# RWKV-7 branch of a two-layer hybrid trunk: the masked key weights times the values, split by halves of the output tokens

## What is computed

```python
sa = jnp.einsum('bhij,bhj->bhi', s, -kk_t)
s = (s * w_t[:, :, None, :] + sa[..., None] * (kk_t * a_t)[:, :, None, :]
     + v_t[..., None] * k_t[:, :, None, :])
out = jnp.einsum('bhij,bhj->bhi', s, r_t)
```

## Time and profile before

| | |
|---|---|
| median of three runs | 2735.82 us (2730.66 to 2738.97) |
| the profiled execution's own time | 2736.47 us |
| its span, first to last instruction | 2734.5 us |
| TensorE matmul busy | 2616.9 us, 96% |
| TensorE weight load busy (overlaps the matmuls) | 1737.3 us, 64% |
| VectorE busy | 1257.9 us, 46% |
| ScalarE busy | 885.4 us, 32% |
| GpSimd busy | 183.4 us, 7% |
| mean granted TensorE clock | 0.993 |

### The profile page before, as it was taken

One profiled execution on the slowest core, in us unless ns is written; L12 is line 12 of the kernel. 1 busy time (PEld: TensorE's weight loads), 2 busy tenths in 40 slices (PEclk: granted clock), 3 DMA queues, 4 the chain that ended last, 5 costly groups with the idle time before them and its releaser, 6 DMA issues.

```text
span 2734.5 us, 49615 instructions
## 1 busy us (share of the span) xinstructions
PE 2616.9 (96%) x21524; PEld 1737.3 (64%) x21524; DVE 1257.9 (46%) x2465; ACT 885.4 (32%) x1438; POOL 183.4 (7%) x166
## 2 busy tenths in 40 slices
PE   8999999999999999999999999999999999999997
PEld 2585666757566666666656858686766656666665
DVE  1462635535287453323344545463638745342323
ACT  1331414233155544310123243333325544431111
POOL 0000000000000000312220000000000000031222
PEclk9999999999999999999999999999999999999999
DMA  9101011020110100131231010100001010012212
GB/s 338 49 17 65 32 40 57 10 72 18 64 38 25 37 16 22 37 119 62 71 121 54 3 41 10 34 18 26 25 19 40 24 37 16 16 39 69 72 64 81
DMA packets 34694, 136.60 MB, mean 50 GB/s; under 512 B 4464, under 2 KB 4496, under 8 KB 33968
## 3 DMA queue, kind: packets, MB, share of 16 engines
q1 hardware_dynamic: 30816, 112.55, 12.3%
q0 software_dynamic: 3664, 20.88, 2.1%
HBM read 126.43 MB, written 6.98 MB: 49 GB/s over the span
## 4 chain that ended last, share of the span: by engine, by line
PE 84%; DVE 7%; ACT 6%; issue 2%; DMA 1%; POOL 0%; ACTq 0%; SPq 0%; DVEq 0%; POOLq 0%
PE psum L575 82%; PE psum L578 2%; DVE m_nm L2014 1%; DVE tmp L1536 1%; ACT tmp L1239 1%; DVE tmp L1539 1%; DVE acts L1536 1%; ACT tmp L1489 1%; DVE tmp L1547 1%; DMA ring<-units 1%; DVE tmp L1543 1%; ACT L1234 0%; ACT L1230 0%; DVE acts L1539 0%; ACT acts L1239 0%
## 5 line engine op out<-in xcount | busy, mean ns | idle before, releaser
L575 PE MATMUL psum<-hT,ring 128*128 128x512 f32 (+2 forms) x3264 | 944.4, 441 | 13.0 <-DVE hT L1544 7.6
L575 PEld LDWEIGHTS psum<-hT,ring 128*128 128x128 f32 x3264 | 524.4, 192 | 437.7 <-issue 393.2
L575 PE MATMUL psum<-tmp 64*64 64x64 f32 (+9 forms) x10624 | 702.1, 258 | 45.8 <-ACT tmp L1239 12.0
L575 PEld LDWEIGHTS psum<-tmp 64*64 64x64 f32 (+3 forms) x10624 | 552.2, 149 | 162.2 <-issue 57.3
L1239 ACT ACTIVATE tmp<-psum 128x256 f32<-128x256 f32 (+7 forms) x478 | 245.6, 517 | 988.6 <-PE psum L575 913.7
L1239 ACT ACTIVATE acts<-psum 128x640 f32<-128x640 f32 (+4 forms) x206 | 109.5, 532 | 316.7 <-PE psum L575 294.3
L575 PE MATMUL psum<-acts,ring 128*128 128x512 f32 (+1 forms) x768 | 210.8, 434 | 0.0
L1536 DVE TENSOR_TENSOR tmp<-psum,tmp 128x256 f32<-128x256 f32 (+2 forms) x184 | 75.7, 412 | 250.5 <-PE psum L575 203.3
L575 PEld LDWEIGHTS psum<-acts,ring 128*128 128x128 f32 x768 | 118.6, 191 | 94.7 <-issue 92.1
L1536 DVE TENSOR_TENSOR tmp<-tmp,psum 128x320 f32<-128x320 f32 x120 | 56.4, 487 | 264.2 <-PE psum L575 202.1
L1536 DVE TENSOR_TENSOR tmp<-tmp 128x320 f32<-128x320 f32 (+2 forms) x214 | 134.8, 656 | 5.0
(11 more groups left out here) (165 smaller groups left out, 2197.7 us busy)
## 6 DMA issues: line engine op xcount, KB each, us to landing
ring<-units SPq DMA_DIRECT2D x210, 512.0 KB, 3.5
small_sb<-small POOLq DMA_DIRECT2D x2, 2944.0 KB, 11.3
hT<-xT POOLq DMA_DIRECT2D x1, 2560.0 KB, 12.3
tmp<-xT POOLq DMA_DIRECT2D x8, 320.0 KB, 5.0
x_keep<-hT POOLq DMA_DIRECT2D x8, 320.0 KB, 3.8
tmp<-x_keep POOLq DMA_DIRECT2D x8, 320.0 KB, 3.5
yT<-acts POOLq DMA_DIRECT2D x8, 320.0 KB, 3.2
tmp<-masks SPq DMA_DIRECT2D x1, 1536.0 KB, 8.5
```

What stands on the lines that cost most here:

```text
L575: return nc.tensor.matmul(out, lhsT, rhs, start=start, stop=stop, skip_group_check=True)
```

## The change

Each unit's product with 128x128 weights and 64 moving columns becomes two products with 64 weight columns each, one for either half `c` of the output tokens. Where `c == d`, the other half of the input tokens is zero by the mask, and the sum runs over the 64 tokens of the same half; otherwise it runs over all 128. Output, tickets and semaphores stay as they were.

```diff
                             for u in range(4):
                                 d, h = u // 2, u % 2
-                                last = mm(psum[:, at + 64 * u:at + 64 * u + 64], B(s, "AakT")[:, u, :],
-                                          B(s, "TA", 2)[:, d, 64 * h:64 * h + 64], True, True)
+                                for c in range(2):
+                                    cs = slice(64 * c, 64 * c + 64)
+                                    ks = cs if c == d else slice(0, P)
+                                    last = mm(psum[cs, at + 64 * u:at + 64 * u + 64], B(s, "AakT")[ks, u, cs],
+                                              B(s, "TA", 2)[ks, d, 64 * h:64 * h + 64], True, True)
                             last.then_inc(filled.sem, filled.mark(("AV", l, p, s)))
```

## The result

The changed kernel takes 2758.39 us, the median of six runs (2756.26 to 2762.22), against 2736.78 us for the kernel before (2730.66 to 2739.43, six runs). The ratio is 1.0082, 95% interval 1.0069 to 1.0095: 21.6 us slower. 2759.5 was forecast, in a range of 2750 to 2771.

The account below looks back on a forecast made before the run. TensorE was taken to bound the kernel. Drains and half-empty segments add 0.53 us at 32 AVs (+16.9) and 0.85 at 8 (+6.8): 2735.8 + 23.7 = 2759.5 us, range 2753 to 2765, widened to 2750 to 2771.

Parts of the forecast that it names:

- What bounds the kernel: Whole kernel: TensorE's matmuls are busy 2616.9 of 2734.5 us; work added to TensorE in the RWKV-7 stage moves the end.
- What an AV costs now: AV between V1 and V2: 1.18 us, of it 0.15 in, 0.83 for eight records, 0.20 out; 1.04 in chunk 4.
- A drain between 128x64 and 64x64: Inside the new AV: each change between these weight shapes makes the next load wait, taken as 0.15 us.
- B: In the new AV: a matmul over 128 tokens, with 128x64 weights; the drain behind it was taken as 0.15 us.
- no drain (2711): Rival: no drain between shapes of 64 columns, the column halves work side by side, 0.47 us against 1.18; chance 0.06.
- drains one way only (2734): Rival: a drain only from wide to narrow, AV 1.06 us, -3.8 us for 32 AVs, +2.1 in chunk 4; chance 0.06.
- the dearer drain (2771): Rival: each of the six drains in an AV takes 0.20 us, +12 us more than forecast; chance 0.06.
- The sum: New AV 1.71 us against 1.18 at 32 places, 1.89 against 1.04 at 8: +16.9 + 6.8 = +23.7 us.
- Six segments behind them, 6 x 0.105: In the new AV: six stretches of same-shape products, each behind a drain, 0.105 us each, 0.63 together.
- the last A: AV's final 64x64 product, on rows 64 to 127; may run beside following blocks, giving back up to 0.1 x 40 us.
- one step to the next block, 0.06: End of the new AV: 0.06 us until the block that follows, counted in the 1.71 us.
- Nothing hidden: Waits at Ye, Yb and after stand behind AV and move with it, so nothing was taken off for them.

## Why the prediction was right

**What bounds the kernel: right.** The period differences came through to the end (the table has both), and the waits of the earlier trace rows did not change.

**What an AV costs now: right,** and the experiments that replaced it by other shapes gave the times that this reading implies.

**A drain between 128x64 and 64x64: right, in both orders.** The earlier trace rows had shown one. The 240 changes in the changed kernel took 0.148 to 0.152 us. For B behind 64 moving columns I chose 0.15 between bounds of 0.15 and 0.20; it measured 0.151. So the length of the drain did not go with the 128 rows: 64x64 and 128x64 weights gave 0.15 alike with 64 moving columns. It went with columns: 0.20 behind 128x64 and behind 64x64 with 128 moving columns, and 0.20 behind 128x128 and 64x128 weights with 64 moving columns. The rivals of no drain (2711) and of drains one way only (2734) fall with this, and so does the dearer drain (2771). The rule of the Trainium skill, page "TensorEngine Tiling (Array Packing)", section "Key Properties", that a change of tiling mode drains the array, held for the order that no row had shown.

**The sum: right, with one term mis-sized.** "Six segments behind them, 6 x 0.105" and "one step to the next block, 0.06" counted the last A in full. It starts beside the next block, 0.007 us ahead of it, and 0.10 of that comes back as a later start of V3. From V1's last record to V2's first it takes 164.20 - 162.64 = 1.56 us, and not the 1.7 that the text gave as a sign; with the 0.10 behind it, the AV between V1 and V2 measured +0.48 against +0.53. The AV of chunk 4 measured +0.82 against +0.85 (from the last load of the projection before AV to the first load behind N, 234.11 to 236.69, where it was 233.03 to 234.79). A pair of heads gives 2.70 against 3.0, and the whole +21.6 against +23.7. The text had given up to 0.1 x 40 = 4 us for this overlap; it was worth 2.

**Nothing hidden: right for the waits that it looked at.** They stayed at 1.0, 0.5 and 0.4 us. It did not look at the short wait before V3 for VectorE, which the earlier trace rows don't list; through this one the late corner came back.

## What to carry to other kernels

Before a product is cut to skip zeros, look at which shapes of weights stand side by side on TensorE, and read in the trace what a change of shape costs from start to start; here it was 0.15 to 0.20 us, more than the 0.11 that the two records of a small product took behind it. Group products by shape, and let those of one shape go to different halves of the array in turn: the same eight products took from 14 us less than the kernel before to 38 us more, by their order alone. Multiplying a block of zeros in the shape of the products beside it can be as fast as leaving it out; here the two orders that did either differed by 0.14 us a pair of heads.

## What the runs showed of the hardware that was not expected

Two products with 64 weight columns each, on different column halves, replaced one with 128 columns at nearly half its price, though nothing was saved in the sum: eight records 0.11 us apart became sixteen in pairs, in 0.46 us (165.03 to 165.64 less the 0.15 out), against 0.83 for the eight. With 64 moving columns and 128 weight columns the loads follow each other at 0.11 us, as long as most matmuls with 128x128 weights and 128 moving columns take in the same trace (0.109 to 0.112); so the weight load, not the multiplication, seems to have set that pace. That is argued and not shown: no run took the load by itself. And a corner of the array that is late by one product didn't hold back the block that started beside it, 0.007 us behind the late one, but the stage that waited, by way of VectorE, for both.
